# Expert rows added to their tokens by one-hot products on TensorE, in place of a scatter and rows read back

## What is computed

```python
h = modulate(rmsnorm(x, norm_ffn[layer]), sh_f, sc_f)
y = hier_moe(h, ...)                       # below
x = x + g_f[:, None, :] * y

def hier_moe(h, ...):                      # t = 512 tokens, d = 1024
    # group by argmax, two experts of the group by top_k, gates: a weight for each
    # 2 t = 1024 assignments (token, expert, weight), sorted by expert, in blocks
    xs = h[row_tok]                        # gathered token rows
    ys = (silu(xb @ w_gate[e]) * (xb @ w_up[e])) @ w_down[e]   # hidden 512
    return zeros.at[row_tok].add(ys * row_w[:, None])
```

## Time and profile before

| | |
|---|---|
| median of three runs | 1883.42 us |
| the profiled execution's own time | 1881.18 us |
| its span | 1879.4 us |
| PE busy | 1525.5 us (81%) |
| VectorE busy | 518.6 us (28%) |
| ScalarE busy | 371.5 us (20%) |
| POOL busy | 87.5 us (5%) |
| moved by DMA | 548.02 MB |

### The profile page before, as it was taken

How to read it: one execution, slowest core, us unless ns; L and a number is a source line. 1 busy time by engine, 2 the same in 40 slices (tenths; PEclk the granted TensorE clock), 3 DMA queues, 4 the chain that set the end, 5 groups by cost and what they waited for, 6 DMA issues and landing times.

```text
span 1879.4 us, 16819 instructions
## 1 busy us (share of the span) xinstructions
PE 1525.5 (81%) x6488; PEld 683.1 (36%) x6488; DVE 518.6 (28%) x1182; ACT 371.5 (20%) x916; POOL 87.5 (5%) x95
## 2 busy tenths in 40 slices
PE   5999998988866776784699999998888847847855
PEld 2455555443322222231244455444433312312311
DVE  2575565350000010010576122224610100000103
ACT  3123344221110010010210144332311101001100
POOL 1000001110000000000000000001110000000000
PEclk9999998999988887897799999998998978978987
DMA  9961723269999999999766112030399999999996
GB/s 357 347 248 52 267 90 137 91 260 373 424 427 417 420 429 413 408 428 417 290 210 198 40 45 90 0 111 28 139 401 423 428 428 426 425 423 422 425 423 285
DMA packets 109589, 548.02 MB, mean 292 GB/s; under 512 B 8876, under 2 KB 46205, under 8 KB 83902
## 3 DMA queue, kind: packets, MB, share of 16 engines
q1 hardware_dynamic: 79808, 492.85, 64.5%
q0 software_dynamic: 12288, 36.41, 5.1%
q10 hardware_dynamic: 17406, 17.59, 2.9%
HBM read 530.37 MB, written 28.34 MB: 297 GB/s over the span
## 4 chain that ended last, share of the span: by engine, by line
PE 58%; DMA 34%; DVE 4%; issue 2%; ACT 1%; SPq 0%; ACTq 0%; POOL 0%; DVEq 0%; POOLq 0%
DMA ring<-in_moe_w_up_dram 13%; PE psum L2179 12%; PE psum L1725 9%; PE psum L1933 9%; DMA ring<-in_moe_w_down_dram 9%; DMA ring<-in_moe_w_gate_dram 7%; PE psum L2212 6%; PE psum L1903 3%; PE psum L1780 3%; DMA T<-in_moe_w_up_dram 2%; DVE W L1098 1%; PE psum L2038 1%; PE psum L1754 1%; DMA V<-xn_scratch,tok 1%; PE psum L1916 1%
## 5 line engine op out<-in xcount | busy, mean ns | idle before, releaser
L2179 PE MATMUL psum<-ring,V 128*32 128x512 f32 (+2 forms) x1712 | 433.2, 668 | 162.7 <-DMA ring<-in_moe_w_up_dram 68.0
L2179 PEld LDWEIGHTS psum<-ring,V 128*32 128x32 f32 (+2 forms) x1712 | 143.7, 144 | 390.0 <-issue 383.5
L2212 PE MATMUL psum<-ring,V 128*32 128x512 f32 (+2 forms) x768 | 199.5, 671 | 68.2 <-DMA ring<-in_moe_w_down_dram 48.7
L993 ACT ACTIVATE V<-psum,modall,scls 128x128 f32<-128x128 f32 x216 | 81.3, 457 | 475.4 <-PE psum L2157 475.4
L1098 DVE SCALAR_TENSOR_TENSOR W<-ring,cact,W 128x512 f32<-128x512 f32 (+1 forms) x224 | 138.4, 618 | 7.7
L2179 PE MATMUL psum<-XN,V 128*32 128x512 f32 (+1 forms) x208 | 109.4, 687 | 21.1 <-DMA ring<-in_moe_w_gate_dram 13.6
L1520 DVE TENSOR_TENSOR V<-V,psum 128x512 f32<-128x512 f32 x28 | 19.3, 688 | 378.2 <-PE psum L2179 378.2
L2212 PEld LDWEIGHTS psum<-ring,V 128*32 128x32 f32 (+2 forms) x768 | 61.3, 142 | 161.6 <-issue 161.6
L1725 PE MATMUL psum<-HT,ring 128*128 128x512 f32 x256 | 117.2, 604 | 0.0
L1536 DVE SCALAR_TENSOR_TENSOR HT<-psum,slot_gate,W 128x512 f32<-128x512 f32 x56 | 42.0, 751 | 249.6 <-PE psum L2212 249.6
L2212 PE MATMUL psum<-XN,V 128*32 128x512 f32 (+2 forms) x192 | 99.2, 667 | 12.0 <-DMA ring<-in_moe_w_down_dram 10.6
(11 more groups left out here) (318 smaller groups left out, 1672.2 us busy)
## 6 DMA issues: line engine op xcount, KB each, us to landing
ring<-in_moe_w_up_dram SPq DMA_DIRECT2D x54, 2048.0 KB, 26.5
ring<-in_moe_w_gate_dram SPq DMA_DIRECT2D x53, 2048.0 KB, 24.0
ring<-in_moe_w_down_dram SPq DMA_DIRECT2D x48, 2048.0 KB, 21.1
ring<-in_ada_w_dram SPq DMA_DIRECT2D x16, 2048.0 KB, 15.2
XN<-in_moe_w_down_dram SPq DMA_DIRECT2D x12, 2048.0 KB, 21.7
ring<-in_ada_w_dram ACTq DMA_DIRECT2D x16, 1024.0 KB, 5.3
XN<-in_moe_w_gate_dram SPq DMA_DIRECT2D x7, 2048.0 KB, 25.7
XN<-in_moe_w_up_dram SPq DMA_DIRECT2D x6, 2048.0 KB, 21.5
```

The lines of the kernel that those rows point to most:

```text
L993: ins = act.activation(V[:, 2 * D + b * D + k * P:2 * D + b * D + (k + 1) * P], bank[0][:, q * P:(q + 1) * P], ACT.Identity, bias=mod[:, 2 ...
L2179: ins = pe.matmul(bank[2 + 2 * i + b][half * w:(half + 1) * w, :], V[:, col:col + w], slot3(x)[:, k, :], start=(k == 0), stop=(k == KC - 1))
L2212: ins = pe.matmul(bank[6 + hf][half * w:(half + 1) * w, :], V[:, col:col + w], slot3(x, 4)[:, k, hf * HALF:(hf + 1) * HALF], start=(k == 0 ...
```

## The change

1. Every column's rows are added to the tokens by products (`token_sums`). For each column VectorE makes a one-hot matrix of 128 rows by 512 tokens in one comparison (`pick`), PE makes eight products with it right behind down(p), and VectorE adds each result to X (`add_sum`). For columns 0 to 12 the results go through two PSUM banks in turn (`sum_bank`); product number c from the third on waits for the add of product c-2. The last column keeps its eight banks, but its adds of the first half no longer wait for products of the second.
2. The clears, the scatters and the reading back are gone, with the semaphores for them.
3. Gathers go two columns ahead, into two parts of V, instead of four ahead. There is one buffer for the hidden rows and one for their transposes, instead of two.
4. HT, which is free thereby, is one more home for weights: eight in layer 0, nine in layer 1.

```diff
-HOMES = (7, 8)
+HOMES = (8, 9)
...
-            return ring[:, SLOT[n], :] if SLOT[n] < RING else (XN, T)[SLOT[n] - RING][:, :]
+            return ring[:, SLOT[n], :] if SLOT[n] < RING else (XN, HT, T)[SLOT[n] - RING][:, :]
...
+        XR = [V[:, D * i:D * (i + 1)] for i in range(2)]
+        HIDDEN, HIDDEN_T = V[:, 4 * D:4 * D + HALF], V[:, 4 * D + HALF:5 * D]
+        Y = V[:, 5 * D:6 * D]
+        PICK = [W[:, 2048:2560], W[:, 512:1024]]
+        TOKENS = W[:, 2560:3072]
+
+        def sum_bank(p, hf, c):
+
+            if p == NB - 1:
+                return bank[((2, 3, 4, 5), (0, 1, 6, 7))[hf][c]]
+            return bank[(2, 4)[c % 2] + p % 2]
...
@@ SP
-                rows_back(l)
...
@@ POOL
                 for p in range(NB):
                     b = p % 2
-                    if p + GATHERED < NB:
+                    if p + 2 < NB:
                         pool.wait_ge(*s["xr_pe"](p * 2 + 2))
-                        gather(tok[:, column(p + GATHERED)], p, s["gath"][p % GATHERED].sem)
-                    if p < NB - 1:
-                        pool.wait_ge(*s["y_evac"](p * 2 + 2))
-                        scatter(dst[:, column(p)], b, s["scat"][b].sem)
+                        gather(tok[:, column(p + 2)], b, s["gath"][b].sem)
...
@@ VectorE
+                def pick(p):
+
+                    if p >= 2:
+                        dve.wait_ge(*s["sum_pe"](2 * TC * (p - 1)))
+                    dve.tensor_scalar(PICK[p % 2], TOKENS, token[:, COLS[p]:COLS[p] + 1], None, ALU.is_equal).then_inc(s["picks"].sem, 1)
...
+                def add_sum(p, hf, c):
+
+                    cols = slice(hf * HALF, (hf + 1) * HALF)
+                    if p == 0:
+                        dve.wait_ge(*s["y_added"](2 * TC))
+                    else:
+                        dve.wait_ge(*s["summed"](2 * TC * (p - 1) + TC * hf + c + 1))
+                    dve.wait_ge(*s["sum_pe"](2 * TC * p + TC * hf + c + 1))
+                    return dve.tensor_tensor(x3[:, c, cols], x3[:, c, cols], sum_bank(p, hf, c), ALU.add)
...
+                hidden(0)
                 for p in range(NB - 2):
-                    hidden_t(p, p % 2)
-                    hidden(p + 1, (p + 1) % 2)
-                    if p < NB - 3:
-                        y_out(p, p % 2)
+                    hidden_t(p)
+                    pick(p)
+                    hidden(p + 1)
+                    y_out(p)
+                    if p == NB - 3:
+                        hidden_t(NB - 2)
+                        pick(NB - 2)
+                    add_sums(p)
...
@@ PE
                     for i, kind in enumerate("gu"):
+                        if p >= 2:
+                            pe.wait_ge(*s["summed"](2 * TC * (p - 2) + 7 + i))
...
+                def token_sums(p):
+
+                    pe.wait_ge(*s["picks"](p + 1))
+                    for hf in range(2):
+                        pe.wait_ge(*s["y_evac"](2 * p + hf + 1))
+                        for c in range(TC):
+                            if p < NB - 1 and hf * TC + c >= 2:
+                                pe.wait_ge(*s["summed"](2 * TC * p + hf * TC + c - 1))
+                            pe.matmul(sum_bank(p, hf, c), PICK[p % 2][:, c * P:(c + 1) * P], Y[:, hf * HALF:(hf + 1) * HALF],
+                                      start=True, stop=True).then_inc(s["sum_pe"].sem, 1)
...
                     if p < NB - 2:
                         gate_up(p + 1, between=p)
                         down(p)
+                        token_sums(p)
```

More of the change, by code:

```diff
@@ L657, in _ @@
                 pool.wait_ge(*s["tok_ready"](1))
-                for p in range(GATHERED):
+                for p in range(2):
                     gather(tok[:, column(p)], p, s["gath"][p].sem)
@@ L1029, in _ @@
                             act.wait_ge(*o["gu_pe"](e * 2 + (2 * u0 + 1)))
-                            act.activation(four(V[:, 4 * D:4 * D + HALF]), by_fours(bank[2]), ACT.Silu).then_inc(o["silu"].sem, 1)
+                            act.activation(four(HIDDEN), by_fours(bank[2]), ACT.Silu).then_inc(o["silu"].sem, 1)
         @block.vector
@@ L1523, in hidden_t @@
+                def hidden_t(e):
                     dve.wait_ge(*s["hid_pe"](e + 1))
-                    if e >= 2:
-                        dve.wait_ge(*s["dn_pe"](e * 2 - 2))
-                    dve.tensor_copy(V[:, 5 * D + b * HALF:5 * D + (b + 1) * HALF], bank[1][:, :]).then_inc(s["hid_t"].sem, 1)
-                def y_out(p, b, hfs=range(2)):
+                    if e:
+                        dve.wait_ge(*s["dn_pe"](e * 2))
+                    dve.tensor_copy(HIDDEN_T, bank[1][:, :]).then_inc(s["hid_t"].sem, 1)
@@ L1545, in _ @@
-                y_out(NB - 3, (NB - 3) % 2, range(1))
-                hidden_t(NB - 2, (NB - 2) % 2)
-                y_out(NB - 3, (NB - 3) % 2, range(1, 2))
-                y_out(NB - 2, (NB - 2) % 2)
-                hidden(NB - 1, (NB - 1) % 2)
-                hidden_t(NB - 1, (NB - 1) % 2)
+                        dve.scalar_tensor_tensor(Y[:, cols], bank[6 + hf], slot_gate[:, COLS[p]:COLS[p] + 1],
+                                                 gf_row[:, cols], ALU.mult, ALU.mult).then_inc(s["y_evac"].sem, 1)
@@ new lines, in _ @@
+                hidden(0)
+                for p in range(NB - 2):
+                    hidden_t(p)
[6 more added lines that the diff above has]
+                    add_sums(p)
+                y_out(NB - 2)
+                add_sums(NB - 2)
+                pick(NB - 1)
+                hidden(NB - 1)
+                hidden_t(NB - 1)
@@ L1552, in add_rows @@
+                y_out(NB - 1)
                 def add_rows(c, signal, at):
@@ L1611, in _ @@
                 for c in range(TC):
-                    dve.wait_ge(*s["add_pe"](TC + c + 1))
-                    for hf in range(2):
-                        cols = slice(hf * HALF, (hf + 1) * HALF)
-                        ins = dve.tensor_tensor(x3[:, c, cols], x3[:, c, cols], bank[LAST_BANKS[hf][c]], ALU.add)
-                    ins.then_inc(s["x_new"].sem, 1)
+                    add_sum(NB - 1, 0, c).then_inc(s["summed"].sem, 1)
+                for c in range(TC):
+                    add_sum(NB - 1, 1, c).then_inc(s["x_new"].sem, 1)
+                    dve.wait_ge(*s["summed"](2 * TC * (NB - 1) + c + 1))
                     dve.wait_ge(*s["x_new"](c + 1))
@@ L2274, in _ @@
                     pe.wait_ge(*o["y"](2 * OV_ROUNDS * E))
[L2276 to L2284 removed]
+                token_sums(NB - 1)
 N_VEC = 5 + 4 + 4 + 3
```

130 lines of the change are left out of this document (45 added, 85 removed).

## The result

The changed kernel takes **1837.6 us** (median of 4 runs, 1835.5 to 1839.8); the kernel before, on the same chip, 1884.2 (1880.9 to 1887.5). The ratio is 0.9746, with a 95% interval of 0.9728 to 0.9764. It is 17 us faster than forecast, outside the range. The profiled execution took 1839.16 us for a span of 1837.3.

The account below looks back on a forecast made before the run. The weight stream was taken to bound both expert stages. Terms of -(10.3+2.6-1+1.9) for layer 0 and -(10.3+1.9) for layer 1 summed to -26.0 us, giving 1855 us; the forecast's own range was 1848 to 1862, eight in ten 1847 to 1876.

Parts of the forecast that it names:

- +1 for late homes: End of layer 0's stage: first down block waits for a free home, 0 to 4 us lost, taken as 1.
- What bounds the kernel: Both expert stages: the weight stream saturates the DMA engines (share 0.99 to 1.00) while TensorE idles 141 us in each.
- Scatters: Expert stages: removing 13 scatters a layer saves their DMA time at 2.46 to 2.63 us per MB, about 10.3 us per layer.
- One more home: Layer 0: the extra weight buffer closes the DMA hole between 440 and 445 us, -2.6 us; layer 1's ninth home, 0.
- Rows read back: End of each stage: these reads queue behind the last weights and delay none, so dropping them gains 0.
- The tail: End of each layer: first four adds run during the last products, one add follows the last product, -1.9 us each.
- The rest: Span outside the two expert stages: forecast to shrink by 3.8 us.
- The sets, and whether they fit: Expert stages: each added set takes 7.6 us of TensorE against room of 9.7, so it fits beside the stream.
- TensorE becomes the bound: Rival, expert stages: each us of a set above 9.7 costs 13 us per layer; 1959 us at low clock; chance 0.10.
- Starvation: Rival, expert stages: late home releases cost 2 us in each of six stretches, +12, 1867 us; chance 0.12.
- scatters for free: Rival, expert stages: scatter packets only filled gaps between weight packets, so 1876 us; chance 0.07.
- Clears, gathers two ahead, one hidden buffer, VectorE: Clears before the stages, the rest within them: DMA has slack, gathers land early, waits and VectorE's work fit; 0 each.

Follow-up runs that it names:

- thinner sets in layer 1: Changed kernel with layer 1's new sets but the last cut to one column in place of 512: 1843.8 us, ratio 0.9784.
- both parts undone: Changed kernel with seven and eight homes again and 13 scatters a layer back as traffic from the gate row: 1873.5 us, ratio 0.9945.

## Why the prediction was wrong

The mechanism was right: a stage lasts as long as its weight stream, and the change shortens the stream. What failed is the size of two terms of the sum, the home (-2.6, and +1 for late homes) and the scatters (-10.3 a layer). Together they were to take 11.9 us from layer 0's stage and 10.3 from layer 1's. Measured, undoing both costs 20.4 and 14.9 us, and all else in the change 2.0 and 1.3.

*What bounds the kernel*: right. The stream does, before and after; thinner sets in layer 1 change nothing.

*Scatters*: the right mechanism at too low a price. The megabytes (4.0 a layer) were right. The 2.46 to 2.63 us per MB from the earlier trace rows is what packets take on the engines, and not what the stage pays: 13.7 and 14.1 us in layer 1 and 13.9 in layer 0 instead of 10.3. Missing were holes and, as I read it, the uneven end. Only in layer 0 without the extra home, as in the kernel before, is the price 9.9, near the forecast. The fabric ceiling of the Trainium skill (DMA: Bandwidth & Descriptors, Where 436 GB/s comes from), which would have made it less still, is the wrong kind of figure here.

*One more home*: this term failed most. I priced one hole, -2.6 and +1 for late homes. Measured: -10.5 alone, -6.5 beside scatters. The hole near 440 was wider than the 5 us that I looked at; without the home TensorE's lateness behind the sets opens a second one before the last four-expert column; and the bulk runs at 425 in place of 427 GB/s. My +1 for late homes in layer 0 was right in kind: the changed kernel has a hole of some 1.2 us at 850 to 860.

*The sum of the stages*: -18.4 and -13.6 against -11.9 and -10.3, 9.8 us of the 16.

*Rows read back, 0*: they took no bytes from the last weights, as argued. But in layer 0 they, and layer 1's first attention weights issued behind them from 903.21 us, filled the DMA engines while TensorE took the branch (4.72 us of issue, then 9.43). With old homes, scatter traffic and no rows read back, layer 0's end is 23.2 us, against 31.2 before; 1.7 of that is the tail, and no run takes the rows alone away. The changed kernel has 27.8, as weights issued early take the rows' place: its stand is 4.57 us. *The tail's* -1.9 was right for what it counted: from the start of layer 1's last products to the last add it is 9.8 us before and 7.9 after. Up to the end of the span only 1.2 are left of it; layer 0's end gained 3.5.

*The rest*, -10.0 against -3.8: 4.4 us are one part of layer 1's attention, at another clock without any edit there, which could not be forecast. That is luck of the profiled execution; without it the 16 us would be about 12.

*The sets, and whether they fit*: right, 7.87 for 7.6. They are hidden in layer 1, and in layer 0 within the 2.0 us above. The room was overstated, 8.9 for 9.7 in layer 0. *TensorE becomes the bound*: the threshold is real and the slope of 13 us per us in layer 0 too; the clock did the opposite of what this rival feared, 0.965 in place of 0.908 over the span, and of the sets only layer 0's last was below full clock (0.81), after its stand. The rule of the Trainium skill on depth-cycling banks (TensorE: Matmul & The Clock Gate, A second HAM failure mode: psum-queue depth-cycling), which it states for a bf16 kernel, isn't borne out here by 13 sets of float32 a layer over two banks.

*Starvation* and *scatters for free*: no. The stream starved less than before, not more; without the extra home it does starve, by the second hole.

*Clears, gathers two ahead, one hidden buffer, VectorE*: 0 each. No run takes them apart; with both parts undone the stages are 2.0 and 1.3 us longer than before, and that is all that they and the sets cost there.

## What to carry to other kernels

Where a stream bounds a stage, price a change by the stage's length at full pace plus its holes, and look for holes over the whole stage, with GB/s to three digits: "share 1.00" hid 5 us, and two causes shared holes, so they didn't add. Small writes among large reads cost more than their bytes: here 13.7 to 14.1 us for 4.0 MB that the stream moves in 9.4. And look at what runs on the DMA engines when an engine takes a branch: a load that is issued early and isn't needed yet can lengthen it.

## What was unexpected of the hardware

HBM's counter of written bytes was 28.34 MB before and 6.32 after, 22.0 less. The 26 scatters are 13.63 of that (19.95 MB with them), which is 26 x 128 rows of 4 KB: it counts dropped rows too. The run in which all rows were dropped shows the same 19.95 MB, yet its queue has 20.00 MB and its stages are 2.7 us longer together. So that counter is no price.

A branch whose body is skipped, with the load of its flag, cost TensorE 2.0 us with the DMA engines idle or at a share of 0.36, and 4.6 with full ones (1.05). And TensorE, relieved of nearly all columns of layer 1's sums, did what was left at 0.86 of the clock in place of 0.97.
